# First mixer's attention: where the scores, the exponentials, the normalisation and the weight rounding stand in each engine's order

## The chip, the cores and the metric

The kernel runs on one core of one Trainium2 chip. The metric is the device time of one execution in microseconds; the median of three runs before the change is 3117.79 us (3117.67 to 3118.09). The core has engines with a program order each: TensorE (PE, with its weight loads shown apart as PEld), VectorE (DVE), ScalarE (ACT), GpSimd (POOL) and the queue that starts the DMAs (SP). They meet only through semaphores.

## The reference, cut to what matters

The program is two transformer blocks on 512 tokens of width 1024. The first block begins with a mixer: a normalised input is projected to queries, keys, values, four pooling groups and two gates of width 1024; the attention is over windows of 128 positions, with a sink logit per head:

```python
sc = jnp.einsum('bqhgd,bkhd->bhgqk', qi, kb).astype(jnp.float32) * ATTN_SCALE
sc = jnp.where(mask, sc, NEG_INF)
sc = jnp.concatenate([sc, jnp.broadcast_to(sink, sc.shape[:-1] + (1,))], axis=-1)
p = jax.nn.softmax(sc, axis=-1)[..., :-1]
return jnp.einsum('bhgqk,bkhd->bqhgd', p.astype(vb.dtype), vb)
```

There are 16 heads of 64 channels, 2 key/value heads, and 4 blocks of 128 queries, each against 256 keys. After it come the merge with the pooled branch under sigmoid gates, an expert layer, and a second block; the change touches none of them.

## The kernel before, in words

`attention` (L738) covers 121.4 to 280.8 us of the span. It runs 32 steps: step n handles query block n // 8 and head pair n % 8 (the two halves of 64 partitions). Beside the attention it computes the 16 gate tiles (8 for each gate, projections of the same normalised input): one gate tile is 8 chunks of 3 matmuls of 128x512, and a step takes 4 chunks, so a gate tile j is made in the gate parts 2j and 2j+1, and gate parts run two steps ahead of the attention (`AHEAD`).

The order of work is written out by hand for every engine.

TensorE, step n: wait for `probs` of n, four transposes of the probabilities (L846) into one PSUM bank; then the scores of n+2 (L819), which wait until the scores of n have been scaled out of their banks; then the gate part n+2 (L256 to L258); then, after ScalarE has copied the transposed probabilities, the values of n (L859).

VectorE: `scale_and_max(n)` is L872 (scores times scale plus mask, from PSUM into `s`), L877 (row maximum) and L879 (negated maximum against the sink); `normalise(n)` is L885 (denominator), L887 (reciprocal) and L889 (the multiplication of 128x512 probabilities). The order is scale 0, scale 1, and then normalise n, scale n+2.

ScalarE: `exp(n)` is for each half an exponential with its row sum (L907, two instructions in the trace) and the sink's exponential (L909). `gate_out(j)` first rounds the weights of a later gate tile to their high part (`w.high`, L150, 128x1024), then reads the finished gate accumulator (L918). Step n: copy of the transposed probabilities (L926), exp of n+2, at odd n gate_out((n+1)/2), and the copy of the attention output (L932).

GpSimd computes the low part of each weight tile (`w.low`, L158, 128x1024, two inputs in SBUF) as soon as ScalarE's high part is there, and at the start of the stage the pooling branch (L795, L802, L806). SP loads each raw weight tile once GpSimd has split the one two tiles back.

Of the kernel before, what the change touches and what calls it, by code (L numbers as in the profile page):

```python
# [26 lines left out]
DC = D // P  # L27
# [225 lines left out]
def product(pe, acc, w, t, x, start, stop):  # L253

    cols = slice(t * P, (t + 1) * P)
    pe.matmul(acc, w[0][:, cols], x[0], start=start, stop=False)  # L256
    pe.matmul(acc, w[0][:, cols], x[1], start=False, stop=False)  # L257
    return pe.matmul(acc, w[1][:, cols], x[0], start=False, stop=stop)  # L258
# [479 lines left out]
def attention(nc, k, q, keys, vals, masks, zp, yp, xn, ga, gp):  # L738
# [3 lines left out]
    STEPS, GATES, AHEAD = NB * QC, 2 * DC, 2  # L742
    PART = DC * GATES // STEPS
    GATE, SCORE, TURNED, OUT = 0, 2, 6, 7
    with ExitStack() as ctx:
# [19 lines left out]
        def score_bank(n):  # L765
            return SCORE + 2 * (n % 2)
# [4 lines left out]
        def rows(half):  # L771
            return slice(half * HD, (half + 1) * HD)

        def block_of(n):
            return slice(n // QC * P, (n // QC + 1) * P)

        with nc.Block() as block:
            @block.sync
            def _(sp):
                sp.dma_start(inv[:, :, :], k.dram["inv_count"]).then_inc(inv_in, 16)  # L780
                sp.wait_ge(k.boot, 64)
                w = dense.cursor()
                for j in range(GATES):
                    w.load(sp, 0, j, GATES)
# [25 lines left out]
            @block.tensor  # L810
            def _(pe):
                w = dense.cursor()

                def scores(n):
                    c = n % QC
                    if n >= 2:
                        pe.wait_ge(scaled, n - 1)
                    for half in range(2):
                        mm = pe.matmul(ps[:, score_bank(n) + half, 0:2 * P], q[rows(half), c, block_of(n)],  # L819
                                       keys[rows(half), c * NKV // QC, n // QC * P:n // QC * P + 2 * P], start=True, stop=True)  # L820
                    mm.then_inc(scored, 1)

                def gate_part(n):
                    j, first = n * PART // DC, n * PART % DC
                    if first == 0:
                        if j >= 2:
                            pe.wait_ge(gate_read, j - 1)
                        w.slot_wait(pe, 0, j, GATES)
                    for t in range(first, first + PART):
                        mm = product(pe, gate_bank(j), w.weights(j), t, chunk(xn, t), t == 0, t == DC - 1)  # L830
                    if first + PART == DC:
                        mm.then_inc(dense.used, 1)

                scores(0)
                scores(1)
                for n in range(AHEAD):
                    gate_part(n)
                for n in range(STEPS):
                    b, kv = n // QC, n % QC * NKV // QC
                    pe.wait_ge(probs, n + 1)  # L840
                    if n:
                        pe.wait_ge(copied, n)
                    for half in range(2):
                        for kb in range(2):
                            at = half * 2 + kb
                            mm = pe.transpose(ps[:, TURNED, at * P:(at + 1) * P], e[:, n % 2, half, kb * P:(kb + 1) * P],  # L846
                                              consts("ident"))
                    mm.then_inc(turned, 1)
                    if n + 2 < STEPS:
                        scores(n + 2)  # L850
                    if n + AHEAD < STEPS:
                        gate_part(n + AHEAD)
                    pe.wait_ge(copied, n + 1)
                    if n:
                        pe.wait_ge(out, n)
                    for kb in range(2):
                        for half in range(2):
                            at = half * 2 + kb
                            mm = pe.matmul(ps[rows(half), OUT, 0:P], vals[:, b + kb, kv, half, rows(half)],  # L859
                                           pt[:, at * P:(at + 1) * P], start=(kb == 0), stop=(kb == 1))  # L860
                    mm.then_inc(mixed, 1)

            @block.vector
            def _(dve):
                sinks = par("sinks")
                dve.tensor_scalar(nsink[:, :], sinks, -1.0, None, ALU.mult).then_inc(chain, 1)
                link = Count(chain, 1)

                def scale_and_max(n):
                    r, h = slice(2 * n, 2 * n + 2), slice(n % QC * 2, n % QC * 2 + 2)  # L870
                    dve.wait_ge(scored, n + 1)
                    dve.scalar_tensor_tensor(  # L872
                        out=s[:, n % 2, :, :], in0=ps[:, score_bank(n):score_bank(n) + 2, 0:2 * P], scalar=SCALE,
                        in1=masks[:, int(n >= QC):int(n >= QC) + 1, :].to_broadcast([P, 2, 2 * P]),
                        op0=ALU.mult, op1=ALU.add).then_inc(scaled, 1)
                    dve.wait_ge(scaled, n + 1)
                    link.inc(dve.tensor_reduce(mx[:, r], s[:, n % 2, :, :], AXX, ALU.max))  # L877
                    link.wait(dve)
                    dve.scalar_tensor_tensor(out=nm[:, r], in0=mx[:, r], scalar=-1.0, in1=nsink[:, h],  # L879
                                             op0=ALU.mult, op1=ALU.min).then_inc(negmax, 1)  # L880

                def normalise(n):
                    r = slice(2 * n, 2 * n + 2)
                    dve.wait_ge(exps, 4 * (n + 1))
                    link.inc(dve.tensor_tensor(den[:, r], su[:, r], es[:, r], ALU.add))  # L885
                    link.wait(dve)
                    link.inc(dve.reciprocal(rc[:, r], den[:, r]))  # L887
                    link.wait(dve)
                    dve.tensor_tensor(e[:, n % 2, :, :], e[:, n % 2, :, :],  # L889
                                      rc[:, r, None].to_broadcast([P, 2, 2 * P]), ALU.mult).then_inc(probs, 1)  # L890

                scale_and_max(0)
                scale_and_max(1)
                for n in range(STEPS):
                    normalise(n)
                    if n + 2 < STEPS:
                        scale_and_max(n + 2)

            @block.scalar
            def _(act):  # L900
                w = dense.cursor()

                def exp(n):
                    act.wait_ge(negmax, n + 1)
                    for half in range(2):
                        j, head = 2 * n + half, n % QC * 2 + half
                        act.activation(e[:, n % 2, half, :], s[:, n % 2, half, :], ACT.Exp, bias=nm[:, j:j + 1],  # L907
                                       accum_out=su[:, j:j + 1]).then_inc(exps, 1)
                        act.activation(es[:, j:j + 1], par("sinks")[:, head:head + 1], ACT.Exp,  # L909
                                       bias=nm[:, j:j + 1]).then_inc(exps, 1)  # L910

                def gate_out(j):
                    dst, bias = (ga, par("b_ga")) if j < DC else (gp, par("b_gp"))
                    if j == DC:
                        act.wait_ge(pooled, 6 + len(PW))
                    w.high(act, 0, j, GATES)
                    w.done(act, j)
                    act.activation(dst[:, j % DC, :], gate_bank(j), ACT.Identity,  # L918
                                   bias=bias[:, j % DC:j % DC + 1]).then_inc(gate_read, 1)

                exp(0)
                exp(1)
                gate_out(0)
                for n in range(STEPS):
                    act.wait_ge(turned, n + 1)
                    act.activation(pt[:, :], ps[:, TURNED, :], ACT.Copy).then_inc(copied, 1)  # L926
                    if n + 2 < STEPS:
                        exp(n + 2)
                    if (n + AHEAD + 1) * PART % DC == 0 and n + AHEAD < STEPS:
                        gate_out((n + AHEAD + 1) * PART // DC - 1)  # L930
                    act.wait_ge(mixed, n + 1)
                    act.activation(q[:, n % QC, block_of(n)], ps[:, OUT, 0:P], ACT.Copy).then_inc(out, 1)  # L932
        dense.close(GATES, 0)
# [2 lines left out]
class Experts:  # L936
# [5 lines left out]
    STEPS = TB // 4  # L942
# [2155 lines left out]
```

## Time and profile before

| what | value |
|---|---|
| median of three runs | 3117.79 us |
| profiled execution, its time | 3118.62 us |
| its span | 3116.8 us |
| busy: PE, PEld, DVE, ACT, POOL | 2917.9, 2396.5, 1782.3, 1063.6, 1280.3 us |
| granted clock of TensorE, mean over the span | 0.973 of full |

The span is the time from the first to the last instruction in the profiled execution; the execution's own time is 1.8 us more. Busy time is the time in which an engine has an instruction in work; of TensorE it says that matmuls are in flight, not that the array is at its peak. An engine's idle time is put down to what released it.

### The profile page before, as it was taken

How to read it: one execution, taken by the hardware profiler on the slowest of the kernel's cores; microseconds unless marked ns; L12 is line 12 of the kernel's file. 1: busy time of each engine (PE TensorE's matmuls, PEld its weight loads, DVE VectorE, ACT ScalarE, POOL GpSimd, SP SyncE). 2: the span in 40 equal slices, each digit the busy share in tenths (PEclk: the TensorE clock that was granted, in tenths of full speed). 3: DMA queues.
4: the chain of work that ended last, by engine and by line, in shares of the span. 5: the costliest groups of instructions: out<-in, count | busy, mean ns of one | idle time of the engine just before them, and what ended most of it. 6: DMA issues, size and time to landing. Idle time of an engine off the chain costs nothing. (4 is left out here: it accounts for less than half of the span.)

```text
span 3116.8 us, 48973 instructions
## 1 busy us (share of the span) xinstructions
PE 2917.9 (94%) x18460; PEld 2396.5 (77%) x18460; DVE 1782.3 (57%) x2599; ACT 1063.6 (34%) x1664; POOL 1280.3 (41%) x649
## 2 busy tenths in 40 slices
PE   7999989999999999999999999979869967999997
PEld 5766778888888888888888888857669955788775
DVE  1354369874777777067777777753846554433115
ACT  3366333343333333321211211245433444433223
POOL 3622333554444444444444444433334322344442
PEclk9999999999999999999999999989989988999998
DMA  3211222444445544655555555522652101222231
GB/s 114 88 61 55 84 86 91 146 134 130 166 165 192 193 166 167 232 175 191 203 196 183 189 197 196 176 80 76 215 160 52 29 14 54 74 94 99 97 101 68
DMA packets 173745, 404.23 MB, mean 130 GB/s; under 512 B 55344, under 2 KB 55472, under 8 KB 172336
## 3 DMA queue, kind: packets, MB, share of 16 engines
q1 hardware_dynamic: 173616, 402.39, 39.2%
q8 instruction: 96, 1.57, 0.2%
q14 instruction: 33, 0.27, 0.0%
HBM read 318.45 MB, written 83.89 MB: 129 GB/s over the span
## 5 line engine op out<-in xcount | busy, mean ns | idle before, releaser
L158 POOL TENSOR_TENSOR weights_low<-weights_raw,weights_high 128x1024 fp32r<-128x1024 f32 x435 | 1128.8, 2595 | 1584.5 <-ACT weights_high L150 1584.5
L150 ACT ACTIVATE weights_high<-weights_raw 128x1024 fp32r<-128x1024 f32 x435 | 460.7, 1059 | 1633.0 <-PE psum L258 1617.0
L256 PE MATMUL psum<-expert_in_high,weights_high 128*128 128x512 f32 x1152 | 458.9, 398 | 8.4 <-DVE expert_in_low L351 4.8
L257 PE MATMUL psum<-expert_in_low,weights_high 128*128 128x512 f32 x1152 | 450.1, 391 | 0.0
L258 PE MATMUL psum<-expert_in_high,weights_low 128*128 128x512 f32 x1152 | 450.0, 391 | 0.0
L256 PE MATMUL psum<-coefficients_high,weights_high 128*128 128x512 f32 x1024 | 399.3, 390 | 5.9 <-DVE coefficients_low L1219 4.2
L257 PE MATMUL psum<-coefficients_low,weights_high 128*128 128x512 f32 x1024 | 398.9, 390 | 0.0
L258 PE MATMUL psum<-coefficients_high,weights_low 128*128 128x512 f32 x1024 | 398.8, 389 | 0.0
L1219 DVE TENSOR_TENSOR coefficients_low<-activation_in,coefficients_high 128x512 fp32r<-128x512 f32 x128 | 354.8, 2772 | 4.4
L256 PEld LDWEIGHTS psum<-expert_in_high,weights_high 128*128 128x128 f32 x1152 | 217.3, 189 | 56.6 <-issue 8.7
L258 PEld LDWEIGHTS psum<-expert_in_high,weights_low 128*128 128x128 f32 x1152 | 217.0, 188 | 45.6
L257 PEld LDWEIGHTS psum<-expert_in_low,weights_high 128*128 128x128 f32 x1152 | 217.5, 189 | 41.5
L1216 DVE TENSOR_TENSOR coefficients_high<-activation_in,table_group 128x512 fp32r<-128x512 f32 x128 | 88.6, 692 | 263.2 <-PE psum L258 263.2
L1200 DVE TENSOR_TENSOR second_key_weighted<-st_and_second_key_onehot,choices 128x512 f32<-128x512 f32 x128 | 223.2, 1744 | 19.4 <-DVE st_and_second_key_onehot L1196 2.4
L256 PEld LDWEIGHTS psum<-coefficients_high,weights_high 128*128 128x128 f32 x1024 | 192.6, 188 | 46.7 <-DVE coefficients_low L1219 4.6
L1196 DVE TENSOR_TENSOR st_and_second_key_onehot<-tables,choices 128x1024 f32<-128x1024 f32 x128 | 159.4, 1245 | 117.0 <-PE psum L1097 102.4
L256 PE MATMUL psum<-mix_in_high,weights_high 128*128 128x512 f32 x472 | 194.7, 412 | 32.8 <-POOL weights_low L113 14.8
L258 PEld LDWEIGHTS psum<-coefficients_high,weights_low 128*128 128x128 f32 x1024 | 192.5, 188 | 40.1
L257 PEld LDWEIGHTS psum<-coefficients_low,weights_high 128*128 128x128 f32 x1024 | 192.6, 188 | 39.9
L257 PE MATMUL psum<-mix_in_low,weights_high 128*128 128x512 f32 x472 | 186.4, 395 | 0.0
L258 PE MATMUL psum<-mix_in_high,weights_low 128*128 128x512 f32 x472 | 186.4, 395 | 0.0
L256 PEld LDWEIGHTS psum<-mix_in_high,weights_high 128*128 128x128 f32 x472 | 90.1, 191 | 69.2 <-issue 30.2
(380 smaller groups left out, 4661.1 us busy)
## 6 DMA issues: line engine op xcount, KB each, us to landing
weights_raw<-in_weights SPq DMA_DIRECT2D x437, 512.0 KB, 3.5
expert_activations<-expert_activation SPq DMA_DIRECT2D x128, 256.0 KB, 4.0
coefficient_table<-table_stage SPq DMA_DIRECT2D x8, 4096.0 KB, 13.2
table_group<-coefficient_table SPq DMA_DIRECT2D x128, 256.0 KB, 4.1
activation_in<-expert_activations SPq DMA_DIRECT2D x128, 256.0 KB, 3.6
chunk_b_k_v<-scan_vectors SPq DMA_DIRECT2D x8, 768.0 KB, 6.1
scan_vectors<-scan_stage SPq DMA_DIRECT2D x4, 1280.0 KB, 6.7
scan_vectors<-scan_stage SPq DMA_DIRECT2D x4, 1024.0 KB, 6.1
```

The lines of the kernel that those rows point to most:

```text
L150: act.activation(d.hi[:, m % SPLIT, :], d.raw[:, m % RAW, :], ACT.Copy).then_inc(d.high, 1)
L158: pool.tensor_tensor(d.lo[:, m % SPLIT, :], d.raw[:, m % RAW, :], d.hi[:, m % SPLIT, :].bitcast(F32), ALU.subtract).then_inc(d.split, 1)
L256: pe.matmul(acc, w[0][:, cols], x[0], start=start, stop=False)
L257: pe.matmul(acc, w[0][:, cols], x[1], start=False, stop=False)
L258: return pe.matmul(acc, w[1][:, cols], x[0], start=False, stop=stop)
L1196: dve.tensor_tensor(onehot[:, u, :, :, :], iota[:, None, None, :].to_broadcast([P, 2, QT, NK]), sel[:, 0:2, bass.ds(t, QT)][:, :, :, None] ...
L1200: dve.tensor_tensor(second[:, u, :, :], onehot[:, u, 1, :, :], sel[:, 2, bass.ds(t, QT)][:, :, None].to_broadcast([P, QT, NK]), ALU.mult). ...
L1216: dve.tensor_tensor(by_block(co[0][:, o, :]), by_block(tile), gt, ALU.mult).then_inc(ex.part, 1)
L1219: dve.tensor_tensor(co[1][:, o, :], tile, co[0][:, o, :].bitcast(F32), ALU.subtract).then_inc(ex.coef, 1)
```

## The change

Four orders are changed, and no instruction is added or taken away. On TensorE the scores of n+2 stand behind the values of n instead of behind its transposes. On VectorE normalise(n) stands one place earlier against the scaling: the order is scale 0, scale 1, normalise 0, normalise 1, scale 2, normalise 2, scale 3 and so on. On ScalarE exp(n+1) stands in step n where exp(n+2) stood. The rounding of a weight tile is taken out of `gate_out` and put, at even n, between the copy of the transposed probabilities and exp(n+1); `gate_out(n/2)` follows that exp, at even n instead of odd n.

```diff
@@ -846,8 +846,6 @@
                             mm = pe.transpose(ps[:, TURNED, at * P:(at + 1) * P], e[:, n % 2, half, kb * P:(kb + 1) * P],
                                               consts("ident"))
                     mm.then_inc(turned, 1)
-                    if n + 2 < STEPS:
-                        scores(n + 2)
                     if n + AHEAD < STEPS:
                         gate_part(n + AHEAD)
                     pe.wait_ge(copied, n + 1)
@@ -859,6 +857,8 @@
                             mm = pe.matmul(ps[rows(half), OUT, 0:P], vals[:, b + kb, kv, half, rows(half)],
                                            pt[:, at * P:(at + 1) * P], start=(kb == 0), stop=(kb == 1))
                     mm.then_inc(mixed, 1)
+                    if n + 2 < STEPS:
+                        scores(n + 2)
 
             @block.vector
             def _(dve):
@@ -891,10 +891,11 @@
 
                 scale_and_max(0)
                 scale_and_max(1)
-                for n in range(STEPS):
+                normalise(0)
+                for n in range(1, STEPS):
                     normalise(n)
-                    if n + 2 < STEPS:
-                        scale_and_max(n + 2)
+                    if n + 1 < STEPS:
+                        scale_and_max(n + 1)
 
             @block.scalar
             def _(act):
@@ -913,21 +914,21 @@
                     dst, bias = (ga, par("b_ga")) if j < DC else (gp, par("b_gp"))
                     if j == DC:
                         act.wait_ge(pooled, 6 + len(PW))
-                    w.high(act, 0, j, GATES)
                     w.done(act, j)
                     act.activation(dst[:, j % DC, :], gate_bank(j), ACT.Identity,
                                    bias=bias[:, j % DC:j % DC + 1]).then_inc(gate_read, 1)
 
                 exp(0)
-                exp(1)
-                gate_out(0)
                 for n in range(STEPS):
+                    j = n * PART // DC
                     act.wait_ge(turned, n + 1)
                     act.activation(pt[:, :], ps[:, TURNED, :], ACT.Copy).then_inc(copied, 1)
-                    if n + 2 < STEPS:
-                        exp(n + 2)
-                    if (n + AHEAD + 1) * PART % DC == 0 and n + AHEAD < STEPS:
-                        gate_out((n + AHEAD + 1) * PART // DC - 1)
+                    if n * PART % DC == 0:
+                        w.high(act, 0, j, GATES)
+                    if n + 1 < STEPS:
+                        exp(n + 1)
+                    if n * PART % DC == 0:
+                        gate_out(j)
                     act.wait_ge(mixed, n + 1)
                     act.activation(q[:, n % QC, block_of(n)], ps[:, OUT, 0:P], ACT.Copy).then_inc(out, 1)
         dense.close(GATES, 0)
```

## Rows read from the trace of the kernel before

**Rows 1.** The page's first line, and the longest wait of TensorE in 121 to 281 us.

```profile
span 3116.8 us, 48973 instructions
...
PE psum L846 <- DVE probabilities L889: 2.6, 2, 1.7
```

**Rows 2.** Timeline (start us, length us, engine, line), TensorE's weight loads, one step.

```profile
185.11 0.42 PEld L846 LDWEIGHTS psum<-tables,probabilities 128*128 128x128 f32 x4 [0.17 <-issue]
...
185.70 0.30 PEld L819 LDWEIGHTS psum<-keys_by_kv_twice,q_then_attention_out 64*128 64x128 f32 x4 [0.17 <-issue]
...
186.33 0.19 PEld L256 LDWEIGHTS psum<-mix_in_high,weights_high 128*128 128x128 f32 x1 [0.33 <-issue]
...
189.28 0.42 PEld L859 LDWEIGHTS psum<-probabilities_transposed,values_by_token 128*64 128x64 f32 x8 [0.35 <-issue]
...
189.87 0.42 PEld L846 LDWEIGHTS psum<-tables,probabilities 128*128 128x128 f32 x4 [0.17 <-issue]
```

**Rows 3.** The same timeline and step, ScalarE and VectorE.

```profile
185.80 0.60 ACT L926 ACTIVATE probabilities_transposed<-psum 128x512 f32<-128x512 f32 x1 [0.30 <-PE psum L846]
...
186.45 0.69 DVE L872 SCALAR_TENSOR_TENSOR scores<-psum,mask_first_and_other 128x512 f32<-128x512 f32 x1 [1.98 <-PE psum L819]
...
188.09 0.51 ACT L907 ACTIVATE probabilities<-scores,negated_max 128x256 f32<-128x256 f32 x1 [1.69 <-DVE negated_max L879]
...
188.37 0.69 DVE L889 TENSOR_TENSOR probabilities<-probabilities,reciprocal 128x512 f32<-128x512 f32 x1
...
189.28 0.28 ACT L909 ACTIVATE sink_exp<-params,negated_max 128x1 f32<-128x1 f32 x1
...
189.47 1.04 ACT L150 ACTIVATE weights_high<-weights_raw 128x1024 fp32r<-128x1024 f32 x1
...
190.41 0.67 ACT L918 ACTIVATE gate_attention<-psum,params 128x512 f32<-128x512 f32 x1
```

**Rows 4.** Timeline, the transposes of the last two steps.

```profile
275.55 0.42 PEld L846 LDWEIGHTS psum<-tables,probabilities 128*128 128x128 f32 x4 [0.17 <-issue]
...
278.06 0.42 PEld L846 LDWEIGHTS psum<-tables,probabilities 128*128 128x128 f32 x4 [0.17 <-issue]
```

**Rows 5.** Timeline, GpSimd's weight split in the step of rows 2.

```profile
190.59 2.39 POOL L158 TENSOR_TENSOR weights_low<-weights_raw,weights_high 128x1024 fp32r<-128x1024 f32 x1 [7.13 <-ACT weights_high L150]
```

**Rows 6.** Timeline from 130.70 us, the first steps: VectorE, GpSimd, TensorE's transposes.

```profile
130.70 0.42 PEld L846 LDWEIGHTS psum<-tables,probabilities 128*128 128x128 f32 x4 [1.27 <-DVE probabilities L889]
...
131.77 2.39 POOL L158 TENSOR_TENSOR weights_low<-weights_raw,weights_high 128x1024 fp32r<-128x1024 f32 x1
...
132.04 0.69 DVE L872 SCALAR_TENSOR_TENSOR scores<-psum,mask_first_and_other 128x512 f32<-128x512 f32 x1 [1.39 <-PE psum L819]
...
134.10 1.32 DVE L885 TENSOR_TENSOR denominator<-row_sum,sink_exp 128x2 f32<-128x2 f32 x1
...
134.13 1.28 POOL L802 TENSOR_TENSOR pooled<-window_sums_a,gate_pool 128x512 f32<-128x512 f32 x1
...
135.37 1.26 POOL L802 TENSOR_TENSOR pooled<-window_sums_b,gate_pool 128x512 f32<-128x512 f32 x1
...
135.46 0.17 DVE L887 RECIPROCAL reciprocal<-denominator 128x2 f32<-128x2 f32 x1
...
135.66 1.52 DVE L889 TENSOR_TENSOR probabilities<-probabilities,reciprocal 128x512 f32<-128x512 f32 x1
...
137.23 0.42 PEld L846 LDWEIGHTS psum<-tables,probabilities 128*128 128x128 f32 x4 [1.95 <-DVE probabilities L889]
...
145.06 5.47 POOL L806 TENSOR_TENSOR pooled<-pooled,pool_in 128x512 f32<-128x512 f32 x4
...
151.72 0.42 PEld L846 LDWEIGHTS psum<-tables,probabilities 128*128 128x128 f32 x4 [0.17 <-DVE probabilities L889]
```

**Rows 7.** Busy time, granted clock (PEclk) and DMA in stretches of 2 us.

```profile
124.00:126.00 2.00, 2.00 (x6) 1.52 (x6) 1.97 (x3) 0.66 (x3) 1.92 (x2) 0.50 0.92 377
...
136.00:138.00 2.00, 0.77 (x6) 0.60 (x8) 1.18 (x1) 0.07 (x1) 2.00 (x2) 1.00 0.40 156
```

## The prediction

> **What bounds the kernel now.** I read the page first for the span, then the waits of TensorE over the attention stage, then the timeline of one step in the middle of it. The page gives a span of 3116.8 us, and the profiled execution's time is 3118.62 us, 1.8 us around the span. In the stage (121.4 to 280.8 us) the longest single entry of TensorE's waits is 2.6 us in two times, on L889, the last instruction of `normalise` [rows 1]. So nearly all of the 32 steps are bound by TensorE itself. In the timeline the reader sees it: transposes start at 185.11 and again at 189.87, a step of 4.76 us, with the gate part from 186.33 to 189.28 (2.95), values 0.59, and transposes and scores 1.22 together; no gap is put down to another engine [rows 2]. I call the start of the transposes of step n T(n). ScalarE and VectorE run ahead: exp(n+2) is done before the step is over, and normalise(n+1) comes right behind the scaling of n+2, on exponentials a step old [rows 3]. The stage is bound by TensorE because the chain of softmax has a whole step of lead.
>
> **What the change does to the lead.** It removes and adds no instruction and no DMA, so TensorE's 4.76 stays its floor. Its groups now come as transposes, gate, values, scores. The boundaries between unlike groups are of the same kind as before (the marks of 0.17 to 0.35 in rows 2); one new pair, scores ahead of transposes, I cost at 0, with 0.1 either way in the steps that TensorE bounds. What changes is that the probabilities of n+1 are now made inside step n: turned(n), copy, exp(n+1), normalise(n+1), transposes of n+1. That chain has to fit into 4.76.
>
> **Odd n (no rounding).** The scores of n+1 now end just before T(n). Before, L872 started 1.34 after the transposes did (185.11 to 186.45), of which transposes and scores are 1.22; so it starts 0.1 after the scores' end, and now 0.1 after T(n) [rows 2, 3]. From L872 to the exponential is 1.64 (186.45 to 188.09). From the exponential to the end of the second sink exponential is 1.19 + 0.28 = 1.47 [rows 3]. normalise is about 0.2 for the denominator, 0.20 from reciprocal to multiplication (135.46 to 135.66, rows 6) and 0.69 [rows 3], 1.1 together, and a hand-over is about 0.05 (L889 ended at 137.18, transposes at 137.23, rows 6). Sum 0.1 + 1.6 + 1.5 + 1.1 + 0.1 = 4.4 to 4.5: just under 4.76, TensorE still sets it. Behind a delayed step the scores are older, L872 starts right at T(n), and the sum is 4.3.
>
> **Even n (rounding of a weight tile).** The copy starts at T+0.69 (185.11 to 185.80) [rows 2, 3]. It holds ScalarE for 0.50 (0.60 less the 0.10 by which L150's 1.04 exceeds its distance of 0.94 to L918). The rounding starts at T+1.19, exp(n+1) at T+2.13, and ends at T+3.60. Without anything more, normalise and hand-over give T+4.75 to 4.80: on TensorE's floor. But the rounding also releases GpSimd: its split starts 1.12 after the rounding does (189.47 to 190.59) and lasts 2.39 [rows 3, 5], so here from T+2.31 to T+4.70. normalise(n+1) falls into the middle of it.
>
> **What such a meeting costs** stands in the first steps [rows 6]. L885 works on 2 columns and takes 1.32 there: it starts at 134.10, GpSimd's L802 runs from 134.13 to 135.41, and L885 ends at 135.42. L889, issued at 135.66, meets the next L802 (135.37 to 136.63) and takes 1.52 instead of 0.69. L872, which reads the scores from PSUM, takes its ordinary 0.69 at 132.04 although a split runs from 131.77. So a VectorE instruction with two inputs in SBUF waits for the end of GpSimd's instruction. The Trainium skill (GPSIMD Engine Reference, Key points) says that GpSimd shares its SBUF interfaces with VectorE and that they contend when VectorE's instruction has two SBUF inputs, but gives no length; if both only went at half speed, the even step would lose about 0.4 in place of what follows, and the whole about 9 us. The rows show the full wait.
>
> So at even n: L885 ends at about T+4.71, L887 starts 0.05 and L889 0.25 behind the split's end (135.41, 135.46, 135.66), L889 ends at T+4.95+0.69 = T+5.64, and transposes start at T+5.69. **The even step takes 5.69 in place of 4.76, +0.93**; TensorE idles that long, as nothing stands ahead of the transposes any more. Before, the same split began inside the transposes and met only the tail of the scaling. Bounds for this term: +0.04 (no wait) and +1.6 (both L885 and L889 wait for something, each as in rows 6: 1.15 + 0.83 over their free lengths, L887's 0.17 for two columns and 0.69, less the 0.4 of slack in an odd step). I take 0.93, as the split's place is fixed by ScalarE's own order, 1.3 us ahead of L885.
>
> **Other queues.** gate_out(j) at even n reads a tile finished in step n-1 and the next user of that bank comes two steps later: no wait. Splits stand ready for a tile at T(n)+4.7 and are needed at T(n+2)+0.6, 5 us later. SP's load follows the split and is needed 16 us later. All at 0; the cover of 5 us is far.
>
> **Head (steps 0 to 3).** T(0) = 130.70 stays: before it only exp(1) and the rounding leave, and normalise 0 was behind the scaling of 1 anyway. T(1): rounding at 131.89, exp(1) at 132.83 to 134.30, split 133.01 to 135.40, L885 to 135.40, L889 then behind an L802 to 136.65, ending 137.20; T(1) = 137.25 against 137.23 [rows 6]. So the head stall does not go: it becomes another meeting. T(2): scaling of 2 meets the third L802 (ends 139.55), exp to 141.07, T(2) = 142.24. T(3): split to 146.95, then L889 behind the first of the four L806 (5.47 / 4 = 1.37 each, rows 6), T(3) = 148.9. T(4): L879 behind a later one to 151.4, T(4) = 154.1 against 151.72: **+2.4**.
>
> **Middle.** Even n from 4 to 28 are 13 steps: 13 x 0.93 = **+12.1**. Odd ones at 4.76.
>
> **Tail.** Before, T(31) - T(30) = 2.51 (278.06 less 275.55), because exp(31) was long done [rows 4]. Step 30 has no gate part, but exp(31) now stands in it behind rounding and copy: 5.65 to 5.69. **+3.1**. The rest of step 31 is unchanged.
>
> **Sum** 2.4 + 12.1 + 3.1 = 17.6. The span goes to 3134.4, the execution's own time to 3136.2; the median of the runs is 0.8 below the profiled execution, so 3117.79 + 17.6 = 3135.4. Own range: the even term 0.7 to 1.1 (-3.0, +2.2), group boundaries 15 x 0.1 = 1.5 either way, head 1.5 either way, the tail's clock -2 to +2: 3130 to 3140.
>
> **Rivals.** (1) *No meeting: VectorE goes on beside GpSimd.* Place: normalise(n+1) at even n; price +0.04 a step (4.80 against 4.76). It decides if L885 and L889 keep 0.15 and 0.69 under a split. Head: T(1) would be 135.46, 1.8 earlier than now. Sum: -1.8 + 15 x 0.04 + tail (4.80 - 2.51 = 2.3) = +1.1, less up to 1.5 if the new boundaries are shorter: 3117.4 to 3118.9, not slower. Against it are the three meetings in rows 6. Chance 0.10. A gain above 0.2% (6.2 us; less than this is what a measurement here can't tell from no change) would need 0.2 off every step's groups, of which no row gives a sign: 0.02 within this.
> (2) *TensorE's clock falls in the new idle.* Place: the gate part behind each stall. The row of 124 to 126 us has the clock at 0.50 (1.2 GHz) after the idle ahead of the stage; 2 us at that level lose 1 us of work. If each of 14 stalls brought it: +14, 3149. Against: the stretch 136 to 138 has TensorE busy 0.77 of 2 us and the clock at 1.00 [rows 7]. Chance 0.07. The Trainium skill (TensorE: Matmul & The Clock Gate, "Why this matters for your kernels") likewise holds that idle time between bursts takes the array to its lower clock; by that rule the tail, idle about 4 us in step 30, is the likelier place, and it would cost 1 or 2 us there.
> (3) *Interfaces shared, not held*: the even step +0.4, head +1, tail +2.6: about +9, 3127. Against: L885 lasted exactly until L802 ended. Chance 0.08.
> (4) *The odd steps don't fit either*: the chain of 4.4 is 0.3 or more longer by waits that I don't see, 15 x 0.2 = 3 more, 3138; within the forecast's upper part. Chance 0.07.
> Forecast as worked out: 0.68.
>
> **Numbers.** 3135.4. Rivals 1 and the low end of 3 lie below the range of 3127 to 3141, rival 2 above. Faster 0.02; same 0.11 (rival 1 with the lowest cases of 3); slower 0.87.
>
> **What the profile after would show.** Transposes at even-to-odd distance 5.7 and odd-to-even 4.76; TensorE's wait on L889 about 14 x 0.93 + head + tail, some 20 us; L885 at about 1.1 us in half of the steps, ending with the split; L889 at its 0.69 there; TensorE's clock at 1.00 within the stage; T(31) - T(30) near 5.7; stages after it the same length. I am wrong if even steps stand at 4.8 (rival 1), at 5.2 (3), or if odd ones exceed 4.8 (4), or if gate matmuls after a stall come at twice their distance (2).

## The result, and the profile after

The changed kernel takes 3134.49 us (median of 5, 3132.8 to 3137.75) against 3118.09 of the kernel before, a ratio of 1.005 with a 95% interval of 1.0038 to 1.0062. Its profiled execution took 3132.8 us, 14.1 us of span more than that of before; it is the shortest of the five.

The page's first line, and TensorE's longest wait in the attention stage (121 to 300 us):

```profile
span 3130.9 us, 48974 instructions
```

```profile
PE psum L846 <- DVE probabilities L889: 22.4, 18, 3.6
```

The 2.6 us of [rows 1] have become 22.4 us in 18 times. One even step and the odd one behind it, in the timeline (start us, length us, engine, line); L910 is the sink exponential:

```profile
186.20 0.42 PEld L846 LDWEIGHTS psum<-tables,probabilities 128*128 128x128 f32 x4 [0.33 <-issue]
...
187.39 1.05 ACT L150 ACTIVATE weights_high<-weights_raw 128x1024 fp32r<-128x1024 f32 x1
...
188.52 2.37 POOL L158 TENSOR_TENSOR weights_low<-weights_raw,weights_high 128x1024 fp32r<-128x1024 f32 x1 [7.87 <-ACT weights_high L150]
...
189.51 0.28 ACT L910 ACTIVATE sink_exp<-params,negated_max 128x1 f32<-128x1 f32 x1
...
189.82 1.08 DVE L885 TENSOR_TENSOR denominator<-row_sum,sink_exp 128x2 f32<-128x2 f32 x1 [1.90 <-ACT sink_exp L910]
...
190.94 0.17 DVE L887 RECIPROCAL reciprocal<-denominator 128x2 f32<-128x2 f32 x1
...
191.14 0.69 DVE L889 TENSOR_TENSOR probabilities<-probabilities,reciprocal 128x512 f32<-128x512 f32 x1
...
191.88 0.42 PEld L846 LDWEIGHTS psum<-tables,probabilities 128*128 128x128 f32 x4 [1.46 <-DVE probabilities L889]
...
192.27 0.19 PEld L256 LDWEIGHTS psum<-mix_in_high,weights_high 128*128 128x128 f32 x1
...
196.44 0.42 PEld L846 LDWEIGHTS psum<-tables,probabilities 128*128 128x128 f32 x4 [0.33 <-issue]
```

From transposes to transposes the even step (186.20 to 191.88) is 5.68 us and the odd one (191.88 to 196.44) 4.56; before, both were 4.76 [rows 2]. The reader sees the reason in L885: two columns in 1.08 us, from 189.82 to 190.90, where GpSimd's split (188.52, 2.37 long) ends at 190.89. The reciprocal and the multiplication, in their ordinary lengths, follow, and the transposes 0.05 behind. L885 was free to start at 189.82, when the last sink exponential was done (189.79): it was no semaphore that held it. So the engines do not meet through semaphores alone, as the opening has it: a VectorE instruction with two inputs in SBUF also meets GpSimd there. The second thing to see is at 192.27: the gate part's first weight load starts 0.39 behind the transposes' first one. Behind the scores it came 0.63 after these, and these 0.59 behind the transposes [rows 2].

The starts of the transposes give the sum by stretches, in the profiled executions of before and after. The stage itself begins 0.58 later than before (T(0) at 131.28, before 130.70), which is part of the last row:

| stretch | before | after | difference | predicted |
|---|---|---|---|---|
| T(0) to T(4), head | 21.02 | 24.18 | +3.2 | +2.4 |
| T(4) to T(30), middle | 123.83 | 133.20 | +9.4 | +12.1 |
| T(30) to T(31), tail | 2.51 | 5.65 | +3.1 | +3.1 |
| T(31) to the first pooling matmul (L728) | 2.78 | 3.56 | +0.8 | 0 |
| pooling matmuls to the first up-projection | 5.96 | 4.56 | -1.4 | 0 |
| all else, by subtraction from the span | | | -1.0 | 0 |

In the head one thing was not in the sum. Busy time, granted clock (the column behind the five engines), DMA share and GB/s in stretches of 2 us, and the timeline around them:

```profile
147.47 5.44 POOL L806 TENSOR_TENSOR pooled<-pooled,pool_in 128x512 f32<-128x512 f32 x4
...
147.76 1.52 DVE L889 TENSOR_TENSOR probabilities<-probabilities,reciprocal 128x512 f32<-128x512 f32 x1
...
149.33 0.42 PEld L846 LDWEIGHTS psum<-tables,probabilities 128*128 128x128 f32 x4 [2.29 <-DVE probabilities L889]
...
150.63 1.05 DVE L879 SCALAR_TENSOR_TENSOR negated_max<-row_max,negated_sinks 128x2 f32<-128x2 f32 x1
...
153.61 0.69 DVE L889 TENSOR_TENSOR probabilities<-probabilities,reciprocal 128x512 f32<-128x512 f32 x1
...
155.46 0.42 PEld L846 LDWEIGHTS psum<-tables,probabilities 128*128 128x128 f32 x4 [0.33 <-issue]
```

```profile
148.00:150.00 2.00, 0.67 (x5) 0.67 (x6) 1.97 (x3) 0.00 (x0) 2.00 (x2) 1.00 0.70 211
...
150.00:152.00 2.00, 2.00 (x7) 1.58 (x7) 1.65 (x2) 0.88 (x2) 2.00 (x3) 0.65 0.13 51
...
152.00:154.00 2.00, 2.00 (x6) 1.35 (x5) 0.72 (x3) 1.18 (x6) 0.91 (x1) 0.50 0.00 0
```

The multiplication of probabilities met the pooling branch's L806 (1.52 us), TensorE had nothing from 147.4 to 149.33, and from about 150.6 to 154 its clock is 0.50, 1.2 GHz: step 3 takes 6.13 (149.33 to 155.46) where an odd step takes 4.56. Not all of that is the clock. L879 waited for L806 as well (1.05 instead of 0.16), as the prediction had it, and the next probabilities were ready at 154.30; the transposes would have started about then, so the clock alone cost about 1.1 us here (an estimate from these rows). Behind the later even steps, which leave TensorE idle for 1.06 us, the clock stays at 1.00 and the steps at 5.68 and 4.56.

The last step, where the exponentials of step 31 now lie inside step 30:

```profile
288.66 0.42 PEld L846 LDWEIGHTS psum<-tables,probabilities 128*128 128x128 f32 x4 [0.33 <-issue]
...
292.28 1.05 DVE L885 TENSOR_TENSOR denominator<-row_sum,sink_exp 128x2 f32<-128x2 f32 x1 [1.89 <-ACT sink_exp L910]
...
294.31 0.72 PEld L846 LDWEIGHTS psum<-tables,probabilities 128*128 128x128 f32 x4 [3.89 <-DVE probabilities L889]
```

288.66 to 294.31 is 5.65, where [rows 4] had 2.51. TensorE is idle for 3.65 us of it, and its clock falls at the end of that. Busy times, clock and DMA from 294 to 300 us:

```profile
294.00:300.00 6.00, 4.37 (x15) 2.56 (x16) 1.75 (x4) 3.03 (x7) 0.00 (x0) 0.50 0.29 91
```

This is the +0.8 ahead of the pooling matmuls. In the kernel before the clock fell too, but later (from 279.8 to 286.6 us), so that more of the pooling matmuls ran at 0.50: this is the -1.4.

### The profile page after: what moved, and what is told of

The parts are those of the page before. It is cut to its first block and busy times, and to the rows that moved or that the text cites. A ratio compares the mean times of both kernels' runs of the same rounds, so it can differ in the third digit from the quotient of the medians.

```text
span 3130.9 us, 48974 instructions
## 1 busy us (share of the span) xinstructions
PE 2913.3 (93%) x18460; PEld 2398.3 (77%) x18460; DVE 1794.0 (57%) x2599; ACT 1062.8 (34%) x1664; POOL 1279.7 (41%) x649
## 5 line engine op out<-in xcount | busy, mean ns | idle before, releaser
L256 PE MATMUL psum<-ffn_in_high,weights_high 128*128 128x512 f32 x352 | 138.4, 393 | 4.9 <-DVE ffn_in_low L351 4.9
```

## The experiments

T(n) is the start of the transposes of step n. Each experiment was timed beside the kernel before; the first four share their runs of it (median 3117.25, 21 runs), the last three theirs (3115.87, 8 runs). The changed kernel was not run beside them: its excess over before, 16.4 us, is from its own comparison. So small differences between totals are not read; what an experiment shows is read from its steps.

**1. The changed kernel with a short split** (7/8 of the low part of the stage's weight tiles is left out).

```diff
-                w.low(pool, 0, j, GATES)
+                m = w.slots + j + SPLIT
+                pool.wait_ge(dense.high, m + 1)
+                pool.tensor_tensor(dense.lo[:, m % SPLIT, 0:P], dense.raw[:, m % RAW, 0:P],
+                                   dense.hi[:, m % SPLIT, 0:P].bitcast(F32), ALU.subtract).then_inc(dense.split, 1)
```

> The changed kernel with GpSimd's split of the weight tiles in the attention stage cut to 128 of 1024 columns (7/8 of the low part is left out), everything else and every wait as in the changed kernel. Theory A, VectorE's two-input instructions wait for the end of GpSimd's split: the split now ends about T+2.7, before L885 at T+3.6, so the even step falls from 5.69 to about 4.78 (chain: copy at 0.69, rounding, exponentials to 3.60, normalise 1.1, hand-overs), L885 takes 0.16 everywhere in steady state, odd steps stay at 4.56. 13 x 0.91 + 0.9 in the tail + 2 or 3 in the head less: about 15 us under the changed kernel, 3118 to 3121. Rival B, it is the rounding's own place on ScalarE that makes the even step long: 5.6 to 5.7 stays and the time is within 2 us of the changed kernel. Rival C, both engines share the port and slow down: even step 5.0 to 5.2.

Measured: 3118.76 us, ratio to before 1.0004 (0.9994 to 1.0013). In this kernel's line numbers L853 is the transposes and L892 the denominator:

```profile
189.85 0.42 PEld L853 LDWEIGHTS psum<-tables,probabilities 128*128 128x128 f32 x4 [0.33 <-issue]
...
192.17 0.47 POOL L793 TENSOR_TENSOR weights_low<-weights_raw,weights_high 128x128 fp32r<-128x128 f32 x1 [8.87 <-ACT weights_high L150]
...
193.47 0.16 DVE L892 TENSOR_TENSOR denominator<-row_sum,sink_exp 128x2 f32<-128x2 f32 x1 [1.90 <-ACT sink_exp L917]
...
194.61 0.42 PEld L853 LDWEIGHTS psum<-tables,probabilities 128*128 128x128 f32 x4 [0.54 <-DVE probabilities L896]
```

The split (0.47 us) is over before the denominator is due, which takes 0.16. The even step is 4.76 (189.85 to 194.61) and the odd one 4.57 or 4.58. The rounding keeps its place ahead of the exponentials, so that place costs 0.2 and the split the other 0.92. Theory A holds, B and C fall. The total is that of the kernel before again: what the odd steps save (T(4) to T(30) is 121.3, before 123.8) the last step takes back (4.75, before 2.51).

**2. The changed kernel with the rounding behind the exponentials.**

```diff
-                    if n * PART % DC == 0:
-                        w.high(act, 0, j, GATES)
                     if n + 1 < STEPS:
                         exp(n + 1)
                     if n * PART % DC == 0:
+                        w.high(act, 0, j, GATES)
                         gate_out(j)
```

> The changed kernel with one part undone: the rounding of a weight tile stands behind exp(n+1) again, directly ahead of gate_out, still at even n. Theory A: the even chain (L872 at T+0.12, exponential 1.64 later, 1.47, normalise 1.1) is T+4.4 to 4.5, so the even step is TensorE's 4.56. The split now runs from about T+4.3 to T+6.65 and meets L879 of the odd step (T+6.1): the odd chain gets 0.4 longer, 4.8 to 4.9. A pair of steps is 9.4 (before 9.52, changed 10.25). Against the kernel before: 15 x -0.1, and +1.9 for the last step, whose exponentials still come late: 3116 to 3120. Rival B (no holding of VectorE by GpSimd): 4.56 in both steps, 3113 to 3115. Rival C (the lead itself is what was lost, whatever the split does): even steps stay over 5, above 3125.

Measured: 3119.9 us, ratio 1.0006 (0.9996 to 1.0015). From T(4) on steps are 4.55 to 4.58, except every second odd one, 4.76 or 4.77, and the last:

```profile
162.78 0.42 PEld L846 LDWEIGHTS psum<-tables,probabilities 128*128 128x128 f32 x4 [0.33 <-DVE probabilities L889]
...
165.91 1.04 ACT L150 ACTIVATE weights_high<-weights_raw 128x1024 fp32r<-128x1024 f32 x1
...
167.03 2.38 POOL L158 TENSOR_TENSOR weights_low<-weights_raw,weights_high 128x1024 fp32r<-128x1024 f32 x1 [6.99 <-ACT weights_high L150]
...
167.33 0.42 PEld L846 LDWEIGHTS psum<-tables,probabilities 128*128 128x128 f32 x4 [0.33 <-DVE probabilities L889]
...
168.90 0.53 DVE L879 SCALAR_TENSOR_TENSOR negated_max<-row_max,negated_sinks 128x2 f32<-128x2 f32 x1
...
172.10 0.42 PEld L846 LDWEIGHTS psum<-tables,probabilities 128*128 128x128 f32 x4 [0.55 <-DVE probabilities L889]
```

T(6) to T(7), an even step, is 4.55. The split now starts 0.3 ahead of T(7), ends at 169.41, and L879 (0.53 instead of 0.16) waits for it; that step is 4.77 (167.33 to 172.10). The forecast had 4.8 to 4.9 in every odd step; the meeting is shorter than forecast, since the rounding comes at 3.13 behind T(6) and the split ends 6.63 behind it. Nor does it delay every odd step: behind a delayed one the scores are older and the exponentials earlier (1.50 behind T(4), 1.76 behind T(6)), so the next split is earlier too, and L879 waits less (0.27 in step 5, which takes 4.56). What this version gains in the middle (T(4) to T(30): 119.77, before 123.83) it loses in the head (T(0) to T(4): 23.91 against 21.02; a stall of 2.4 us ahead of T(2) is followed by a clock of 0.50 from 141.7 to 145.1) and in the last step (4.37 against 2.51).

**3. The changed kernel with TensorE's order undone** (scores behind the transposes again).

```diff
                     mm.then_inc(turned, 1)
+                    if n + 2 < STEPS:
+                        scores(n + 2)
                     if n + AHEAD < STEPS:
                         gate_part(n + AHEAD)
...
                     mm.then_inc(mixed, 1)
-                    if n + 2 < STEPS:
-                        scores(n + 2)
```

> The changed kernel with TensorE's order alone undone: scores of n+2 again between the transposes and the gate part. Theory A, the gate part's first weight load may start under the last transpose but not under the scores: the odd step goes back from 4.56 to 4.76, the even step (bound by the chain through the split, 5.69) stays; 13 to 15 x 0.2, 2.5 to 3 us above the changed kernel, 3137. Rival B, the 0.2 came with the idle time or with the scores' new place ahead of the transposes: the odd step stays at 4.56 and the time within 1 us of the changed kernel. Rival C, earlier scores shorten the even chain as well: even step under 5.5 and a faster kernel than the changed one.

Measured: 3137.47 us (3134.92 to 3138.72), ratio 1.006 (1.0045 to 1.0076). Weight loads of TensorE:

```profile
180.87 0.42 PEld L846 LDWEIGHTS psum<-tables,probabilities 128*128 128x128 f32 x4 [1.12 <-DVE probabilities L889]
...
185.63 0.42 PEld L846 LDWEIGHTS psum<-tables,probabilities 128*128 128x128 f32 x4 [0.17 <-issue]
...
186.22 0.30 PEld L819 LDWEIGHTS psum<-keys_by_kv_twice,q_then_attention_out 64*128 64x128 f32 x4 [0.17 <-issue]
...
186.86 0.19 PEld L256 LDWEIGHTS psum<-mix_in_high,weights_high 128*128 128x128 f32 x1 [0.33 <-issue]
...
191.35 0.42 PEld L846 LDWEIGHTS psum<-tables,probabilities 128*128 128x128 f32 x4 [1.13 <-DVE probabilities L889]
```

The odd step is back at 4.76 (180.87 to 185.63), the even one stays at 5.72 (to 191.35). Scores start 0.59 behind the transposes and the gate part 0.64 behind them. So the 0.2 hangs on what stands directly behind the transposes, not on idle time; the scores' earlier place gives the even step nothing. The total alone would not show this: its interval overlaps that of the changed kernel.

**4. The kernel before with the scores ahead of the transposes.** This takes the 0.2 without the short lead.

```diff
                 for n in range(STEPS):
                     b, kv = n // QC, n % QC * NKV // QC
+                    if n + 2 < STEPS:
+                        scores(n + 2)
                     pe.wait_ge(probs, n + 1)
...
                     mm.then_inc(turned, 1)
-                    if n + 2 < STEPS:
-                        scores(n + 2)
```

> The kernel before with one move: the scores of n+2 stand directly ahead of the transposes of n (which is behind the values of n-1) instead of behind them; ScalarE, VectorE and GpSimd as before, exponentials two steps ahead. Theory A: TensorE's groups come as in the changed kernel, so the step is 4.56 in place of 4.76, while normalise(n+1) still works on exponentials that are a step old: it ends by T+3 (behind scaling of n+2, T+0.12 to 1.76), and by T+3.2 where the split holds it, 1.3 ahead of need. 26 steady steps x 0.2 = 5.2, up to 0.5 more at the head, tail unchanged: 3112 to 3114. Rival B, the later scaling (1.3 later against the transposes) makes normalise late behind the split: steps of 4.9 and more, slower than before. Rival C, the 0.2 is bound to the short lead: 4.76, no change.

Measured: 3106.26 us (3104.5 to 3111.99), ratio 0.9965 (0.9952 to 0.9979): faster than both kernels. L848 is the transposes here:

```profile
185.89 0.30 PEld L819 LDWEIGHTS psum<-keys_by_kv_twice,q_then_attention_out 64*128 64x128 f32 x4 [0.17 <-issue]
...
186.52 0.42 PEld L848 LDWEIGHTS psum<-tables,probabilities 128*128 128x128 f32 x4 [0.33 <-issue]
...
186.60 2.41 POOL L158 TENSOR_TENSOR weights_low<-weights_raw,weights_high 128x1024 fp32r<-128x1024 f32 x1 [6.70 <-ACT weights_high L150]
...
188.09 0.94 DVE L879 SCALAR_TENSOR_TENSOR negated_max<-row_max,negated_sinks 128x2 f32<-128x2 f32 x1
...
189.33 0.69 DVE L889 TENSOR_TENSOR probabilities<-probabilities,reciprocal 128x512 f32<-128x512 f32 x1
...
191.07 0.42 PEld L848 LDWEIGHTS psum<-tables,probabilities 128*128 128x128 f32 x4 [0.33 <-issue]
```

Every step of the middle is 4.55 (but the last, 3.92, which has no scores ahead of T(30)), also this one, in which L879 waits 0.8 for the split (186.60 to 189.01): the multiplication of the next probabilities ends at 190.02, 1.05 ahead of the transposes at 191.07. T(0) to T(4) is 18.61, 2.4 less than before: T(0) to T(1) is 4.92 instead of 6.53. There L879 is held to the end of the split (133.04, 1.54 long), L885 behind it is not (134.51, 0.15), and L889 is (134.89, 1.46), where in the kernel before L885 and L889 each lost a whole meeting [rows 6]; the step from T(2) to T(3) is 4.58 instead of 4.96. The gain of the head was in the forecast with 0.5 only, nor was there a word of a further 2.9 between the pooling matmuls and the up-projection (3.11 against 5.96). From the stage's first scores to the first pooling matmul it is 151.1 us against 159.4.

**5. The kernel before with the rounding's place alone.**

```diff
 def gate_out(j):
-                    w.high(act, 0, j, GATES)
...
+                    if n * PART % DC == 0:
+                        w.high(act, 0, n * PART // DC, GATES)
                     if n + 2 < STEPS:
                         exp(n + 2)
```

> The kernel before with one part of the change alone: the rounding of a weight tile stands at even n between the copy of the transposed probabilities and exp(n+2), gate_out stays where it was; TensorE, VectorE and the exponentials' order as before. Theory A, the meeting of split and VectorE costs whatever the lead of the exponentials: the split runs from T+2.3 to T+4.7, L879 (T+2.8) waits for its end, then denominator, reciprocal and the multiplication of n+1 follow in VectorE's order and end about T+5.7, so the even step is 5.75 in place of 4.76. 14 x 1.0, no loss in the last step (exp(31) is a step early): 3129 to 3134. Rival B, the early exponentials of the kernel before give normalise(n+1) the slack to absorb it: steps of 4.76 to 4.85 and within 2 us of the kernel before.

Measured: 3132.22 us (3131.76 to 3134.02), ratio 1.005 (1.0034 to 1.0067).

```profile
187.04 0.42 PEld L846 LDWEIGHTS psum<-tables,probabilities 128*128 128x128 f32 x4 [0.17 <-issue]
...
189.36 2.39 POOL L158 TENSOR_TENSOR weights_low<-weights_raw,weights_high 128x1024 fp32r<-128x1024 f32 x1 [8.14 <-ACT weights_high L150]
...
189.83 1.94 DVE L879 SCALAR_TENSOR_TENSOR negated_max<-row_max,negated_sinks 128x2 f32<-128x2 f32 x1
...
192.07 0.69 DVE L889 TENSOR_TENSOR probabilities<-probabilities,reciprocal 128x512 f32<-128x512 f32 x1
...
192.81 0.42 PEld L846 LDWEIGHTS psum<-tables,probabilities 128*128 128x128 f32 x4 [1.19 <-DVE probabilities L889]
```

The even step is 5.77 (187.04 to 192.81), odd ones 4.75 to 4.77. L879 starts 0.47 into the split and takes 1.94, and the multiplication of the next step's probabilities, whose exponentials are a whole step old, stands behind it in VectorE's order. This one part of the change costs as much as the whole of it.

**6. The changed kernel with the split done twice** (the operands are shortened to lo, raw and hi here).

```diff
+                    pool.tensor_tensor(lo, raw, hi, ALU.subtract).then_inc(again, 1)
+                    pool.wait_ge(again, j + 1)
                     pool.tensor_tensor(lo, raw, hi, ALU.subtract).then_inc(dense.split, 1)
```

> The changed kernel with GpSimd's split of each tile of the attention stage done twice, the second behind the first (same values written). Theory A: L885 slips in between the two, L889 waits for the end of the second at about T+7.1, transposes at T+7.6: the even step grows from 5.69 to 7.6 or 7.7, the odd one stays at 4.56; with head and tail 27 to 32 us above the changed kernel. Rival B, VectorE is only slowed beside GpSimd: even step 6.0 to 6.5. Rival C, the even step is set by ScalarE's rounding and not by the split: 5.7.

Measured: 3185.62 us (a single run, so this total has no interval). L900 is the multiplication, L857 the transposes:

```profile
200.98 2.37 POOL L794 TENSOR_TENSOR weights_low<-weights_raw,weights_high 128x1024 fp32r<-128x1024 f32 x1 [9.05 <-ACT weights_high L150]
...
203.43 2.34 POOL L797 TENSOR_TENSOR weights_low<-weights_raw,weights_high 128x1024 fp32r<-128x1024 f32 x1
...
203.60 2.71 DVE L900 TENSOR_TENSOR probabilities<-probabilities,reciprocal 128x512 f32<-128x512 f32 x1
...
206.37 0.54 PEld L857 LDWEIGHTS psum<-tables,probabilities 128*128 128x128 f32 x4 [3.48 <-DVE probabilities L900]
...
212.53 0.42 PEld L857 LDWEIGHTS psum<-tables,probabilities 128*128 128x128 f32 x4 [0.33 <-issue]
```

```profile
204.00:208.00 4.00, 1.63 (x7) 1.44 (x8) 3.76 (x4) 0.66 (x2) 1.76 (x1) 0.83 0.28 89
...
208.00:212.00 4.00, 4.00 (x21) 2.88 (x19) 1.02 (x3) 1.33 (x6) 0.00 (x0) 0.75 0.10 42
```

The multiplication lasts 2.71 us, until 206.31, 0.54 behind the second split's end at 205.77. The step before is 7.71 (198.66 to 206.37), as forecast. But the time is 51 us over the changed kernel, not 27 to 32, and the reason is in the odd steps: 6.16 (206.37 to 212.53). In the second fence the clock is 0.83 and 0.75 in the 8 us from 204; the weight loads at 206.88 and 207.96 take 0.34 and 0.33 instead of 0.19. TensorE is idle for about 3.1 us ahead of each odd step (here until 206.37), and each time the clock falls in the gate part behind it. From T(5) on the 13 odd steps take 5.90 to 6.16, 1.3 to 1.6 more than in the changed kernel; with 1.1 at T(1) this is the missing 20.

**7. Experiment 4 again**, for the pooling matmuls.

> The same kernel as in the run with the scores ahead of the transposes, once more. That one gained 11 us, of which the trace shows 8.3 in the stage and 2.9 in the eight pooling matmuls behind it, which ran at the full granted clock. If the second part belongs to the kernel (the clock no longer falls at the stage's end), its trace shows about 3.1 us from the first pooling matmul to the first up-projection again, and 10 to 12 us under the kernel before. If it was chance of that execution, 4.5 to 6 us there, and 8 to 9 under the kernel before.

Measured: 3105.8 us (3104.46 to 3107.12), ratio 0.9965 (0.9951 to 0.9979).

```profile
270.64 3.67 PE L728 MATMUL psum<-pooled,pool_group_weights 128*128 128x512 f32 x8 [0.63 <-PEq L777]
...
273.75 0.79 PE L256 MATMUL psum<-ion_out_then_merged_high,weights_high 128*128 128x512 f32 x1
```

Again 3.11 us. The gain is 10.1 us, in experiment 4 it was 11.0, so the second part seems to belong to this kernel; yet experiment 5, 15 us slower, has 3.11 there as well, and the others 4.5 to 6.1. Why the clock holds in some and not in others stays open.

## Why the prediction was right

- *The even step, +0.93*: measured +0.92. The wait of L885 for the split's end was the one mechanism, shown from four sides: shorter split, no wait (experiment 1); another place, another instruction waits (2); the place alone in the kernel before, about the same price, +1.0 a step (5); twice the split, 2 us more (6). The Trainium skill (GPSIMD Engine Reference, Key points) says that the two engines contend where VectorE's instruction has two inputs in SBUF. The trace agrees: L885 took 1.08 us instead of 0.16. The runs show besides that the wait goes to the end of GpSimd's instruction, so that rival 3 (half speed, even step +0.4) falls.
- *The odd step, 4.76*: the term that was mis-sized. The prediction put the new boundaries between unlike groups at 0 with 0.1 either way; the transposes followed by the gate part save 0.20, in 13 steps 2.6 of the 2.7 us by which the middle came out short. Experiments 3 and 4 give the 0.2 back and take it. Rival 1 had said that no row gives a sign of 0.2 off every step's groups; the odd steps had just that.
- *The head, +2.4*: measured +3.2. The stalls at T(1) and T(3) came as meetings with the pooling branch, within 0.2. What was missing is the fall of the clock in step 3: 6.13 where 5.2 was predicted (148.9 to 154.1, by L879 behind L806, which came as worked out).
- *Rival 2, the clock*: it did not come at the 0.93 of each even step, which is what the price of +14 needed, but it came in the head behind the stall at T(3), and behind every stall of 3.1 us in experiment 6. The Trainium skill (TensorE: Matmul & The Clock Gate, "Why this matters for your kernels") holds that idle gaps between bursts of matmuls bring the lower clock. The trace agrees for the stalls of 3.1 us, and for the tail, where the prediction had expected it by that rule: the clock fell at 294.0, in the idle time ahead of T(31). But it had fallen in the kernel before as well, so that against it the stretch from T(31) to the first up-projection changed by +0.8 and -1.4 only. Shorter stalls went either way. The one of 136 to 138 us in the kernel before [rows 7] kept the clock, and so did T(1) of the changed kernel, whose weight loads wait 2.29 us like those of T(3). In experiment 3 an idle time of TensorE of 1.71 us ahead of T(1) kept it, and one of 1.69 us ahead of T(3) was followed by 0.50. So the length of the stall alone doesn't decide; what does is not shown here.
- *The tail, +3.1*: measured +3.1. *Rivals 1 and 4* fall: no even step at 4.8, no odd one over 4.8 outside the head.
- *The sum*: +17.6 predicted, 16.4 by the medians, 14.1 in the profiled executions, where the misses are -2.7 and +0.8 in the stage and +0.8, -1.4 and -1.0 outside it. The mechanism was right; that the total came out so near is in part luck, as these misses partly cancel. T(0), which was to stay, came 0.58 later, and one reading was a little off: in the kernel before the split starts 0.72 behind the transposes (189.87 to 190.59), behind them and not inside; no term hangs on it.

## What to carry to other kernels

When a step is moved, follow what it releases on the other engines: the rounding cost ScalarE nothing new, but it moved GpSimd's 2.4 us split onto VectorE's chain. A lead of one step does not protect work that stands in program order behind an instruction that waits for another engine's instruction to end. And a group order can be had for itself: moving the scores one place forward, with every lead kept, gave the shorter TensorE step without the rest.

## What the runs showed of the hardware that was not expected

- The weight load of the 128x512 products starts 0.39 us behind the first load of four fp32 transposes, but scores start 0.59 behind a group of transposes or of values, transposes 0.59 behind values, and transposes or the gate part 0.63 or 0.64 behind scores: 4.56 or 4.76 a step by order alone.
- An idle time of TensorE of 1.04 to 1.06 us, thirteen times in 124 us, left its granted clock at 1.00. Of two of 1.88 us in the changed kernel one lowered it, of 1.71 and 1.69 us in experiment 3 the shorter one, and fifteen of 3.1 us in experiment 6 did each time, at 1.3 to 1.6 us over a step of 4.56.
- Not every VectorE instruction waits for GpSimd. In the changed kernel, beside L806 (147.47 to 152.91), L872 with its scores from PSUM took 0.68 us and L877 with one input 0.69, as always, while L889 took 1.52 and L879 1.05. The wait goes the other way too: while L889 went on until 137.73, the pooling branch's L802 at 137.14 took 1.74 us, its neighbours 1.26 and 1.30.
